# Four seams between matmul stages of a fused two-block kernel: weaving two chunks, and moving the last quarters of the input off the matrix engine

## The reference

```python
# first block
merged = sigmoid(gate_a) * ya + sigmoid(gate_b) * (yb @ w_proj_b)
h = x + merged @ w_out
z = rmsnorm(h, norm_ffn_g)
h = h + (silu(z @ w_ffn_gate) * (z @ w_ffn_up)) @ w_ffn_down
x = rmsnorm(h, norm_final_g)
# second block
proj = rms_norm(x, norm_g) @ w_in_2        # mem_z, mem_q and eleven more parts
merged = sigmoid(g_conv) * o_conv + sigmoid(g_mla) * o_mla + sigmoid(g_mem) * o_mem
x = x + merged @ w_o
```

## Time and profile before

| | us |
|---|---|
| median of three runs (2494.6 to 2496.9) | 2495.15 |
| the profiled execution | 2497.96 |
| its span, first to last instruction | 2496.2 |

### The profile page before, as it was taken

The page is one execution under the profiler, slowest core; times in us unless marked ns, Lnnn a source line. Parts: engine busy times, 40 slices in busy tenths (PEclk is TensorE's granted clock), DMA queues, the critical chain, the costliest instruction groups (busy, mean ns, idle before and its releaser), DMA issues.

```text
span 2496.2 us, 29562 instructions
## 1 busy us (share of the span) xinstructions
PE 2481.8 (99%) x11286; PEld 2044.6 (82%) x11286; DVE 1566.2 (63%) x2145; ACT 1135.9 (46%) x1441; POOL 343.6 (14%) x676
## 2 busy tenths in 40 slices
PE   9999999999999999999999999999999999999999
PEld 7877778888888888888888788888888888888887
DVE  6766665476656555557656765567667757665664
ACT  5444434444444444444545454444445555545443
POOL 1100020023223211122002001002121000013110
PEclk9999999999999999999999999999999999999999
DMA  9855456677676777666556556566675555467664
GB/s 272 224 172 158 144 169 201 194 230 219 198 222 200 223 203 210 202 210 211 194 194 216 192 182 186 166 182 202 212 208 178 167 167 176 151 194 218 202 212 135
DMA packets 256573, 486.39 MB, mean 195 GB/s; under 512 B 30058, under 2 KB 37392, under 8 KB 256048
## 3 DMA queue, kind: packets, MB, share of 16 engines
q1 hardware_dynamic: 233712, 458.37, 59.8%
q0 software_dynamic: 21504, 22.06, 3.1%
q10 hardware_dynamic: 1216, 4.07, 0.5%
HBM read 459.90 MB, written 2.49 MB: 185 GB/s over the span
## 4 chain that ended last, share of the span: by engine, by line
PE 96%; DVE 2%; ACT 1%; issue 1%; DMA 0%; SPq 0%; DVEq 0%; ACTq 0%
PE acc L598 28%; PE acc L600 27%; PE acc L599 27%; PE banks L874 2%; PE banks L875 2%; PE banks L873 2%; PE acc L873 1%; PE acc L874 1%; PE acc L875 1%; PE banks L681 1%; DVE w_lo L1635 1%; PE banks L1043 0%; PE banks L1020 0%; ACT w_hi L1185 0%; PE banks L950 0%
## 5 line engine op out<-in xcount | busy, mean ns | idle before, releaser
L1635 DVE TENSOR_TENSOR w_lo<-raw,w_hi 128x1024 fp32r<-128x1024 f32 x864 | 1040.3, 1219 | 765.8 <-ACT w_hi L1185 752.0
L1185 ACT ACTIVATE w_hi<-raw 128x1024 fp32r<-128x1024 f32 x864 | 905.1, 1055 | 1136.2 <-PE acc L600 1025.1
L598 PE MATMUL acc<-w_hi,x_hi_A 128*128 128x512 f32 x1880 | 742.8, 395 | 1.4 <-DVE w_lo L1635 1.4
L600 PE MATMUL acc<-w_hi,x_lo_A 128*128 128x512 f32 x1880 | 733.3, 390 | 0.0
L599 PE MATMUL acc<-w_lo,x_hi_A 128*128 128x512 f32 x1880 | 732.5, 390 | 0.0
L598 PE MATMUL acc<-w_hi,x_hi_B 128*128 128x512 f32 (+1 forms) x1216 | 471.8, 388 | 0.1
L600 PE MATMUL acc<-w_hi,x_lo_B 128*128 128x512 f32 (+1 forms) x1216 | 469.9, 386 | 0.0
L599 PE MATMUL acc<-w_lo,x_hi_B 128*128 128x512 f32 (+1 forms) x1216 | 469.8, 386 | 0.0
L598 PEld LDWEIGHTS acc<-w_hi,x_hi_A 128*128 128x128 f32 x1880 | 353.4, 188 | 84.4 <-issue 11.3
L600 PEld LDWEIGHTS acc<-w_hi,x_lo_A 128*128 128x128 f32 x1880 | 353.3, 188 | 74.5
L599 PEld LDWEIGHTS acc<-w_lo,x_hi_A 128*128 128x128 f32 x1880 | 353.8, 188 | 71.8 <-issue 0.5
(11 more groups left out here) (295 smaller groups left out, 1419.9 us busy)
## 6 DMA issues: line engine op xcount, KB each, us to landing
raw<-in_w_in_dram SPq DMA_DIRECT2D x376, 512.0 KB, 4.3
raw<-in_w_ffn_gate_dram SPq DMA_DIRECT2D x88, 512.0 KB, 3.9
raw<-in_w_ffn_up_dram SPq DMA_DIRECT2D x88, 512.0 KB, 4.1
raw<-in_w_ffn_down_dram SPq DMA_DIRECT2D x88, 512.0 KB, 4.6
raw<-in_w_out_dram SPq DMA_DIRECT2D x32, 512.0 KB, 5.0
raw<-in_w_mem_kv_dram SPq DMA_DIRECT2D x32, 512.0 KB, 4.1
raw<-in_w_mla_out_dram SPq DMA_DIRECT2D x32, 512.0 KB, 5.1
raw<-in_w_o_dram SPq DMA_DIRECT2D x32, 512.0 KB, 3.9
```

The costliest lines, as they stand in the source:

```text
L598: mm(o, xh, hi[:, k, :], start=(kt == first_k), stop=False)
L600: last = mm(o, xl, hi[:, k, :], start=False, stop=(kt == (last_k or c.kts) - 1))
L1185: ins = act.activation(w_hi[:, s, 0:n], raw[:, r, 0:n], ACT.Copy)
L1635: ins = dve.tensor_tensor(w_lo[:, s, 0:n], raw[:, r, 0:n], w_hi32[:, s, 0:n], ALU.subtract)
```

## The change

At each of the four seams the first two chunks after the seam are woven: their 16 granules run as granules 0 to 3 of the first chunk (z = 0), 0 to 3 of the second (z = 1), then 4, 5 of each and 6, 7 of each. Quarter 2 is first needed at position 8 and quarter 3 at position 12; the first chunk is complete after 14 granules, the second after 16. SP, TensorE, ScalarE and VectorE all follow this order. Every quarter at these seams now goes the block way: six quarters leave TensorE, `with_turn` and `first_mem_gate` go, and GpSimd gets six more sets of 16 transfers. Buffers for the added blocks (`first_squares`, `xres_squares`, `fin_from`, `total_squares` and theirs) and semaphores are added. The placement of `ask_high`, which lets ScalarE begin a hi part, changes with it: `before` asked for several ahead at k = 2 and 3, `after` asks for each behind the turn of the newest quarter.

```diff
+    def woven(name, *ones):
+        return (name, 1, [c for _, _, cc in ones for c in cc])
...
-    out += [one("w_out", "A", 0, KT, "w_out", k * CW) for k in range(4)]
+    out += [woven("w_out_woven", *(one("w_out", "A", 0, KT, "w_out", k * CW) for k in range(2)))]
+    out += [one("w_out", "A", 0, KT, "w_out", k * CW) for k in (2, 3)]
...
+        both = [one(n, "A", 0, KT, "w_in_2", C2[n] + h * CW) for n in ("ez", "eq")]
+        out += both if h else [woven("mem_woven", *both)]
...
-    out += [one("w_o", "A", 0, KT, "w_o_2", k * CW) for k in range(4)]
+    out += [woven("w_o_woven", *(one("w_o", "A", 0, KT, "w_o_2", k * CW) for k in range(2)))]
+    out += [one("w_o", "A", 0, KT, "w_o_2", k * CW) for k in (2, 3)]
     return out
+
+
+WEAVE = [(z, g) for gs in (range(0, 4), (4, 5), (6, 7)) for z in range(2) for g in gs]
+WOVEN_FIRST, WOVEN_SECOND = 14, 2
+
+
+def granule_order(name, i, chunks):
+
+    if name.endswith("_woven") or (name == "ffn_up" and i == 0):
+        return [(chunks[z], g) for z, g in WEAVE]
...
-            for k in range(2):
+            for k in range(4):
...
-            for k in range(3):
+            for k in range(4):
...
-            for k in range(2):
+            for k in range(4):
                 pool.wait_ge(fin_turned, k + 1)
-                if k:
+                if k == 1:
                     pool.wait_ge(fin_moved[0], 256)
-                move_by_tile(as_rows(fin_to[k]), as_squares(fin_from[k]), fin_moved[k])
+                move_by_tile(as_rows(fin_to[k]), as_squares(fin_from[k]), fin_moved[k % 2])
...
-            def with_turn(c, v, waits=()):
-
-                need(pe, acc_free[C.slot(2)], C.rounds(2))
-                for g in range(c.grans):
-                    if g in waits:
+            def woven(a, b):
+
+                banks = C.slot(2), C.slot(2, 1)
+                for z, g in WEAVE:
+                    if g == 0:
+                        need(pe, acc_free[banks[z]], C.rounds(2, z))
+                    if z == 0 and g % 2 == 0:
                         activations()
-                    if g == 2:
-                        turn_quarter(v)
-                    granule(c, g, C.slot(2))
-                C.n += 1
+                    granule((a, b)[z], g, banks[z])
+                C.n += 2
...
-            for _ in range(3):
+            for _ in range(4):
                 one("proj_b")
-            with_turn(next_one("proj_b"), cols(merged1, 2))
-            with_turn(next_one("w_out"), cols(merged1, 3), (0, 2, 4, 6))
+            woven(next_one("w_out"), next_one("w_out"))
             n, chunks = next((n, cc) for nm, n, cc in SEG if nm == "ffn_up")
-            for k in range(3):
+            for _ in range(2):
                 one("w_out")
-            with_turn(chunks[0], cols(xres, 3), (0, 2, 4, 6))
-            chunk(chunks[1])
+            woven(*chunks)
...
-                    first_mem_gate(next_one("ez"))
+                    woven(next_one("ez"), next_one("eq"))
...
-            with_turn(next_one("w_o"), cols(merged2, 3), (0, 2, 4, 6))
-            for _ in range(2):
-                one("w_o")
+            woven(next_one("w_o"), next_one("w_o"))
+            one("w_o")
...
+            for k in (2, 3):
+                W.ahead(4)
+                act.wait_ge(act_req, W.R.at(1))
+                act.wait_ge(first_moved[k], 256)
+                high_turned("A", first_turn[k], 4 * k)
...
+            W.ahead(6)
+            done_chunk()
+            W.ahead(2)
+            done_chunk()
+
+            def high_residual(k):
+                act.wait_ge(act_req, W.R.at(1))
+                act.wait_ge(xres_moved[k], 256)
+                high_scaled("B", xres_turn[k], 4 * k, GCOL["norm_ffn_g"] + 4 * k)
+            plain()
+            high_residual(0)
+            W.some(2)
+            high_residual(1)
+            plain()
+            high_residual(2)
+            W.ahead(8)
+            high_residual(3)
...
+                if woven:
+                    W.ahead(6)
+                    evac_tanh(gate_c)
+                    done_chunk(gate_c)
+                    W.ahead(2)
+                    done_chunk(up_c)
...
             for k in (2, 3):
-                for kt in (4 * k, 4 * k + 2):
-                    split_unit("A", kt, GCOL["norm_final_g"] + kt)
+                act.wait_ge(fin_turned, k + 1)
                 for t in range(T):
                     ins = act.activation(squared[:, k - 2, t, :], xres[:, t, k * CW:(k + 1) * CW], ACT.Square,
                                          accum_out=sm[:, 4 + 4 * t + k:5 + 4 * t + k])
                 ins.then_inc(squares_done, 1)
                 W.some(1)
+            W.some(1)
+            for k in (2, 3):
+                act.wait_ge(act_req, W.R.at(1))
+                act.wait_ge(fin_moved[k % 2], 512)
+                high_scaled("A", as_turn(fin_to[k]), 4 * k, GCOL["norm_final_g"] + 4 * k)
+                W.ahead(4)
             places += [cols(merged2, k) for k in range(4)]
             for h2 in range(2):
-                gated()
-                if h2:
+                if h2 == 0:
+                    W.ahead(2)
+                    evac_tanh(first_ez)
+                    done_chunk(first_ez)
+                    W.ahead(1)
...
-            for kt in (12, 14):
-                split_unit("A", kt)
-            plain(4)
+            W.ahead(7)
+            act.wait_ge(act_req, W.R.at(1))
+            act.wait_ge(total_moved[1], 512)
+            high_turned("A", total_turn[:, 3], 12)
+            W.ahead(6)
+            done_chunk()
+            W.ahead(2)
+            done_chunk()
...
+            def take_silu(dst, c=None, grans=None):
                 if c is None:
                     W.split_next()
                     c = this()
-                a = ask_tanh(c)
+                a = ask_tanh(c, grans)
                 W.more()
                 STT(dst, etmp[:], 1.0, a[:], ALU.add, ALU.mult).then_inc(acc_free[W.C.slot(2, -1)], 1)
...
-                if k < 2:
-                    turn_blocks(first_squares[k], cols(merged1, k)).then_inc(first_turned, 1)
-                    dve.wait_ge(first_turned, k + 1)
-                else:
-                    ask_quarter()
-                if k == 2:
-                    for _ in range(4):
-                        ask_high()
-                if k == 3:
+                turn_blocks(first_squares[k], cols(merged1, k)).then_inc(first_turned, 1)
+                dve.wait_ge(first_turned, k + 1)
+                if k >= 2:
                     ask_high()
-                    ask_high()
-                if k >= 2:
                     dve.wait_ge(act_done, W.R.next())
                     low_turned("A", first_turn[k - 2], 4 * k - 8)
                     activations()
             for k in (2, 3):
-                for kt in (4 * k, 4 * k + 2):
-                    low_part("A", kt, asked=True)
+                W.ahead(4)
+                ask_high()
+                dve.wait_ge(act_done, W.R.next())
+                low_turned("A", first_turn[k], 4 * k)
                 activations()
...
+
+            def turn_residual(k):
+                turn_blocks(xres_squares[k].rearrange("p t b n -> p b t n"), cols(xres, k)).then_inc(xres_turned, 1)
+                dve.wait_ge(xres_turned, k + 1)
+
+            def low_residual(k, part=None):
+                ask_high()
+                if part is not None:
+                    row_part(xres, part)
+                dve.wait_ge(act_done, W.R.next())
+                low_scaled("B", xres_turn[k], 4 * k, GCOL["norm_ffn_g"] + 4 * k)
+                activations()
+            W.ahead(6)
+            take_add(cols(xres, 0), WOVEN_FIRST)
+            turn_residual(0)
+            W.ahead(2)
+            take_add(cols(xres, 1), WOVEN_SECOND)
+            turn_residual(1)
+            W.some(1)
+            for k in range(2):
                 row_part(xres, k)
-                if k:
-                    dve.wait_ge(act_done, W.R.next())
-                    low_scaled("B", xres_turn[k - 1], 4 * k - 4, GCOL["norm_ffn_g"] + 4 * k - 4)
-                    activations()
-            for kt in (12, 14):
-                low_part("B", kt, GCOL["norm_ffn_g"] + kt, asked=True)
-            activations()
+            take_add(cols(xres, 2))
+            turn_residual(2)
+            low_residual(0)
+            W.some(2)
+            low_residual(1, 2)
+            take_add(cols(xres, 3))
+            turn_residual(3)
+            low_residual(2, 3)
+            W.ahead(4)
...
+            W.ahead(4)
+            low_residual(3)
...
+                if i == 0:
+                    W.ahead(6)
+                    take_silu(hid, gate_c, WOVEN_FIRST)
+                else:
+                    W.split_next()
+                    take_silu(hid, gate_c)
+                    if mem is not None:
+                        ask_high()
+                    W.split_next()
```

(69 more changed lines are left out.)

84 lines of the change are left out of this document (28 added, 56 removed).

## The result

The changed kernel takes **2503.3 us** (median of nine runs, 2501.97 to 2504.95). The kernel before, run nine times beside it, takes 2496.9 (2494.6 to 2497.19); its three runs shown ahead had 2495.15. The ratio is 1.0028, 95% interval 1.0020 to 1.0037: **slower by 0.28%**, 6.4 us. The forecast was 2499.0 with a range up to 2502.0, so the result lies above it. The profiled execution took 2504.22 (span 2502.4).

A forecast was written before the change was run, and what follows sets the result against it. TensorE, busy 99% of the span, was taken as the bound. Seam terms +0.43 + 2.67 + 0.03 - 0.88 = +2.25, with clock +3.85, gave 2501.8 from the profiled 2497.96, so median 2499.0 us; range 2495.0 to 2502.0.

The forecast's parts named there:

- Transposes: All four seams: six quarters' transposes leave TensorE at 0.88 us each, 5.28 us less work.
- D: The fourth seam: one quarter's transposes leave TensorE and no stop appears, -0.88 us.
- A: Seam proj_b to w_out: stop of 3.56 us at position 2, 2.19 more, less 1.76 for two quarters: +0.43 us.
- B: Seam w_out to ffn_up: new stop of 3.55 us at position 16, less 0.88 for one quarter: +2.67 us.
- C: Seam ffn_down to ez/eq: two quarters -1.76, stops +0.96 at the start and +0.83 at the end: +0.03 us.
- GpSimd and the transfers: At the seams: six more sets of 16 transfers, 12.8 us each to land, cost 0, bound 0 to 3 us.
- The clock: Behind the new stops at A and B: one of the two loses full clock, 1.6 us; 0 to 3.2 together.
- Rival 1: Both long stops, at A and at B, lose the clock: +5.45, 2500.6 us, chance 0.22.
- The base: Whole kernel: sum made against the profiled 2497.96 us, then lowered by 2.8 us to the median 2495.15.
- The lower end of the range: Whole kernel: 2495.0 us, the forecast without clock loss and with B's stop half as long.
- rival 2: VectorE or transfers late at C position 8, B position 4 or A's last `proj_b` chunk: +1 to +3, chance 0.13.

The follow-up runs named there:

- b_free_first: Changed kernel with, at B, the gate chunk's multiply ahead of the two splits: 2498.41 us, ratio 1.0006 to the kernel before.
- best4: best2 with, at C, two splits made while ScalarE and VectorE wait for transfers of the final norm's third quarter: 2493.74 us, ratio 0.9987.
- best2: all_stops_out with, at A, the first split of w_out's first chunk made ahead of quarter 1's halves: 2491.93 us, ratio 0.9983.
- after_again: The changed kernel run once more, unaltered, for its records of the clock: 2503.87 us.
- b_split_one: Changed kernel with one split, not two, ahead of the gate chunk's multiply at B: 2499.51 us, ratio 1.0011.
- a_q1_early: Changed kernel with, at A, quarter 1's high and low halves made ahead of the fourth take_add_times: 2499.53 us, ratio 1.0011.
- a_turn_last: Changed kernel with, at A, quarter 1's halves ahead of the last turning of blocks but behind the fourth take: 2502.09 us, ratio 1.0024.
- all_stops_out: Changed kernel with the edits of b_free_first and a_q1_early, plus at C multiply before splits and first split before quarter 2's blocks: 2493.19 us, ratio 0.9986.

## Why the prediction was wrong

By its own steps:

- **Transposes, -5.28.** Right. 48 instructions went, and at D, where nothing else happened, the sum of TensorE's steps beyond 0.227 us fell by 0.93 (0.88 forecast).
- **A, stop of 3.56 at position 2, +0.43.** Right in place, cause and size: 3.74 by the same count. Between 500 and 560 us those steps grew by 2.02; less the half clock, 1.5, that is +0.5.
- **B, stop of 3.55 at position 16, +2.67.** Right: 3.75, released by the multiply L1867. Between 560 and 680 us the growth was 5.45; less 2.8 of half clock, +2.65. b_free_first shows that the stop and the half clock go together when two lines change places.
- **C, +0.03.** Right: stops of 1.45 and 1.04, start to start (0.5 + 0.96 and 0.83 forecast). Over the seam, the steps beyond 0.227 us changed by -0.3 to +0.3 in all, by where the stretch is cut.
- **GpSimd and the transfers, 0.** Right for the time of this kernel, wrong in the reason. A set was put at 16 x 0.54 and its landing, 12.8 us; at C the issues of two sets alone take 26.5 us in best4. In the changed kernel no stop is ended by them. The pause that makes a set longer stood in the trace of before: of the 20 issues in the earlier trace rows the last sixteen take from 603.17 to 615.25, 12.1 us and not 8.6 (rows in the last section).
- **The clock, +1.6.** This is the step that failed. The forecast took "one of the two" stops to lose the clock, for 1.6 us, from the one fall in the earlier trace rows. Both lost it, in every one of the eight times that a stop of 3.6 us stands in a trace, and one of the falls here is twice as long as the one in mid-kernel in the trace of before: 1.5 + 2.8 = 4.3 us. Rival 1 had the mechanism, with 0.22 and 3.2 us; it too took every fall to be as long as the one that the trace held. The row of before showed one length of fall, and nothing said that it was the only one. And two stops of the same length, 3.56 and 3.55, were likely to fare alike; "one of the two" was a mean between two cases and not a case.
- **The base.** The three runs shown had the median 2495.15, and nine 2496.9; the sum, made against a profiled execution of 2497.96, was brought down by 2.8 us where 1.1 was due. The forecast's difference of +3.85 from 2496.9 would have been 2500.8, so of the 4.3 us by which the forecast missed, 1.8 were the base and 2.7 the clock, less 0.1 elsewhere.
- **Smaller slips.** The lower end of the range, without clock and with half of B's stop, comes to 2497.4 - 1.8 = 2495.6 and not 2495.0, and rival 1 with most of rival 2 is more than 0.26.

The sum with what was measured: +0.5 + 2.65 + 0.0 - 0.93 = +2.2, and 4.3 of clock, +6.5 against 6.4 between the medians and 6.3 between the two profiled executions. The Trainium skill's warning against gaps between bursts of matmuls ("TensorE: Matmul & The Clock Gate", section "Why this matters for your kernels") fits the stops of A and B. The traces differ from it at shorter gaps than it warns of: 1.92, 2.25, 2.41 and 2.65 us lost the clock, 2.03 and 2.94 did not.

What the change meant to gain was there, and it was given back at two stops. With the orders mended at A, B and C (best2) it is **faster than before by 0.17%** (0.08 to 0.26%; it is the fastest of several variants, which flatters it a little). The rest of what six quarters are worth is still in C (2.57 of stop and 1.7 of clock in best2's trace), where the transfers that GpSimd sends and the splits behind them are the next bound. That the transfers are the bound there is argued from best4's rows; a kernel with C's transfers issued otherwise was not tried.

## What to carry to other kernels

On an engine that is busy 99% of the time, price a new stop as stop plus clock: in these traces 19 of 22 stops of 1.9 us or more had a fall of 3.4 us or more with them, for 1.5 to 3 us on top. When a consumer is brought nearer to its producer (here by weaving two chunks), go through every queue for what stands between the producer's last input and the instruction that frees the buffer, and put the freeing one first: at B two lines changed places and gave back 5.5 us. And look at what an engine does while it waits for another: at A a split put there closed a stop of 2.2 us. Where the wait is for transfers, as at C, the same move only shifted the stop.

## What the runs showed that was not expected

**A fall of the clock follows a stop of about 2 us or more, not always, and its length varies.** From the twelve traces, past the first 60 us: idle of TensorE and the stretch at half that begins in it or within 1.4 us behind it. 1.20 (made by hand), 1.29, 1.40 and 1.57: none. 1.92: 3.4 us. 2.03: none, twice. 2.25 and 2.41: 3.4. 2.65, 3.38, 4.10, 4.11: 3.4. 2.94 (best4, at C): none. 3.58 (A): 3.4 in the changed kernel and in b_free_first, 6.8 in after_again and b_split_one. 3.60 (B): 6.8 in the changed kernel and in a_q1_early, 3.4 in a_turn_last and after_again. 4.83 and 5.56: 6.8. 6.28 and 7.01: 10.2.

**The fall at 281 us is not part of the kernel.** It stands in the trace of before and in six others, and is missing in five (after_again, a_q1_early, a_turn_last, best2, best4). In a_turn_last:

```profile
281.40:284.80 3.40, 3.40 (x21) 2.94 (x20) 3.17 (x4) 0.18 (x1) 0.00 (x0) 1.00 0.51 145
```

Matmul by matmul, the traces without it are 1.1 us shorter over this stretch than that of the changed kernel: eight steps of 0.43 cost 1.4 more, and 0.3 of it comes back at the next wait. The times bear the size out. Of 69 runs of the kernel before, the 35 with a mean granted clock of 1.000 have the median 2495.69, the 34 with 0.999 have 2497.2; that it is this fall that tells them apart is not shown. Together with the start of the kernel, where the traces of the changed kernels are up to 2.9 us apart at their 500th matmul, this is of the size of the spread between runs (2494.6 to 2498.8), and a reason to count a seam within its own stretch, and not to make a sum against one profiled execution without asking which falls it held.

**GpSimd's issues of small transfers pause.** The sixteen of one set follow each other at 0.53 us; at C, behind the first twelve, the traces of the changed kernel, b_free_first, all_stops_out, best2 and best4 show 4.5 to 5.75 us in which it issues nothing and waits for nothing that the profile names. In the changed kernel at C, and in the kernel before at B:

```profile
1435.47 6.32 POOL L552 DMA_DIRECT2D arena<-arena  x12 [74.51 <-DVE arena L1794]
1447.54 8.42 POOL L552 DMA_DIRECT2D arena<-arena  x16 [5.75 <-issue]
1457.94 2.11 POOL L552 DMA_DIRECT2D arena<-arena  x4 [1.99 <-issue]
...
603.17 6.33 POOL L534 DMA_DIRECT2D arena<-arena  x12 [9.71 <-DVE arena L1754]
613.12 2.13 POOL L534 DMA_DIRECT2D arena<-arena  x4 [3.62 <-issue]
```

So it is nothing that the change brought: in the kernel before, too, sets of `move_by_tile` pause, mostly behind twelve issues, and then for 3.1 to 7.7 us. The sets that `move` sends at D, sixteen of them as well, pause for 0.21 us only. What GpSimd waits for was not found out.
